# Token sums moved from VectorE to GpSimd, and the first block's groups cut as 4, 6, 6 and 6 chunks, in a two-layer diffusion backbone

## What is computed

```
for l in range(DEPTH):                                   # DEPTH = 2
    sh1, sc1, g1, ... = split(silu(c) @ w_mod[l] + b_mod[l])   # nine vectors of 1024, for latents and context
    x   = x   + 0.5 * g1  * swiglu(modulate(x, nw[0], sh1, sc1),   ffn1_up[l], ffn1_down[l])
    ctx = ctx + 0.5 * cg1 * swiglu(modulate(ctx, nw[0], ch1, cs1), ffn1_up[l], ffn1_down[l])
    ... token mixer: gated linear attention and window pooling, gates, w_out ...
    x   = x   + 0.5 * g3  * swiglu(modulate(x, nw[2], sh3, sc3),   ffn2_up[l], ffn2_down[l])
def swiglu(h, w_up, w_down):                             # w_up: 1024 x 5632, w_down: 2816 x 1024
    a, b = split(h @ w_up); return (silu(a) * b) @ w_down
```

## Time and profile before

| what | us |
|---|---|
| median of 3 runs | 2830.38 (2829.36 to 2835.23) |
| the profiled execution's own time | 2831.64 |
| its span from the first to the last instruction | 2829.4 |
| TensorE matmul busy | 2784.5 (98%) |
| VectorE busy | 1962.4 (69%) |
| ScalarE busy | 975.0 (34%) |
| GpSimd busy | 532.4 (19%) |

### The profile page before, as it was taken

One profiled execution on the slowest core, in us unless ns is written; L12 is line 12 of the kernel. 1 busy time (PEld: TensorE's weight loads), 2 busy tenths in 40 slices (PEclk: granted clock), 3 DMA queues, 4 the chain that ended last, 5 costly groups with the idle time before them and its releaser, 6 DMA issues.

```text
span 2829.4 us, 40890 instructions
## 1 busy us (share of the span) xinstructions
PE 2784.5 (98%) x15744; PEld 2472.1 (87%) x15744; DVE 1962.4 (69%) x3220; ACT 975.0 (34%) x1543; POOL 532.4 (19%) x456
## 2 busy tenths in 40 slices
PE   7999999999999999999999999999999999999998
PEld 5899899888888888999999889898988778888886
DVE  4668889565367747988886788888856577563334
ACT  5233224354322233423233433242444332432223
POOL 1013113214500020213132213131331500200000
PEclk9999999999999999999999999999999999999999
DMA  7322433231134423233332323424223145343332
GB/s 244 103 60 81 130 105 86 69 77 45 41 94 124 122 65 101 83 105 107 102 110 83 97 72 89 126 80 131 80 58 91 42 131 153 107 132 104 92 96 79
DMA packets 463787, 275.56 MB, mean 97 GB/s; under 512 B 17610, under 2 KB 461812, under 8 KB 463604
## 3 DMA queue, kind: packets, MB, share of 16 engines
q1 hardware_dynamic: 461396, 269.09, 33.8%
q10 hardware_dynamic: 2208, 4.00, 0.4%
HBM read 270.95 MB, written 2.10 MB: 97 GB/s over the span
## 4 chain that ended last, share of the span: by engine, by line
PE 92%; DVE 3%; ACT 2%; issue 1%; DMA 1%; POOL 0%; SPq 0%; ACTq 0%; DVEq 0%; POOLq 0%
PE ps L1698 37%; PE ps L1712 19%; PE ps L1956 17%; PE ps L1963 9%; PE ps L1924 2%; PE ps L1744 2%; PE ps L1929 1%; PE ps L1039 1%; DMA wraw<-in_ffn_up 1%; PE ps L1019 1%; ACT whi L2054 1%; DVE wlo L2357 0%; ACT hhi L2119 0%; PE ps L1007 0%; DVE hlo L2499 0%
## 5 line engine op out<-in xcount | busy, mean ns | idle before, releaser
L2357 DVE TENSOR_TENSOR wlo<-wraw,whi 128x1024 fp32r<-128x1024 f32 (+2 forms) x299 | 320.3, 1076 | 259.5 <-ACT whi L2054 256.6
L2054 ACT ACTIVATE whi<-wraw 128x1024 fp32r<-128x1024 f32 (+2 forms) x291 | 269.1, 926 | 588.2 <-PE ps L1712 403.4
L1698 PE MATMUL ps<-hhi,whi 128*128 128x512 f32 x1472 | 461.2, 364 | 2.2 <-ACT whi L2054 2.2
L1698 PE MATMUL ps<-hlo,whi 128*128 128x512 f32 x1472 | 453.1, 359 | 0.0
L1712 PE MATMUL ps<-hhi,wlo 128*128 128x512 f32 x1472 | 318.4, 362 | 0.0
L1698 PEld LDWEIGHTS ps<-hhi,whi 128*128 128x128 f32 x1472 | 245.9, 189 | 48.6 <-ACT whi L2054 3.8
L1712 PEld LDWEIGHTS ps<-hhi,wlo 128*128 128x128 f32 x1472 | 244.1, 188 | 44.6 <-issue 3.2
L1698 PEld LDWEIGHTS ps<-hlo,whi 128*128 128x128 f32 x1472 | 245.4, 188 | 42.8 <-issue 0.5
L2989 POOL TENSOR_TENSOR ssum<-wraw 128x512 f32<-128x512 f32 x52 | 73.1, 1406 | 1014.4 <-PE ps L1963 367.5
L1698 PE MATMUL ps<-mhi_fast,whi 128*128 128x512 f32 (+1 forms) x912 | 236.3, 340 | 1.4 <-DVE mlo_fast L2814 1.4
L1698 PE MATMUL ps<-mlo_fast,whi 128*128 128x512 f32 (+1 forms) x912 | 234.6, 338 | 0.0
(11 more groups left out here) (310 smaller groups left out, 5709.6 us busy)
## 6 DMA issues: line engine op xcount, KB each, us to landing
wraw<-in_ffn_up SPq DMA_DIRECT2D x176, 512.0 KB, 4.2
wraw<-in_w_in SPq DMA_DIRECT2D x64, 512.0 KB, 4.1
wraw<-in_ffn_down SPq DMA_DIRECT2D x80, 384.0 KB, 4.5
wraw<-in_w_mod SPq DMA_DIRECT2D x68, 256.0 KB, 3.1
modraw<-in_w_mod SPq DMA_DIRECT2D x32, 512.0 KB, 3.7
modraw_down<-in_w_mod SPq DMA_DIRECT2D x30, 512.0 KB, 3.7
flow_first<-in_w_mod SPq DMA_DIRECT2D x86, 128.0 KB, 4.2
first_mod<-in_w_mod SPq DMA_DIRECT2D x8, 1024.0 KB, 12.0
```

The costliest lines, as they stand in the source:

```text
L1698: nc.tensor.matmul(o, whi[:, slot, k, :], a[:, k * NT + t0:k * NT + t0 + n], start=(k == 0 and a is hi), stop=False)
L2054: nc.scalar.activation(whi[:, slot2, k, n], wraw[:, slot4, k, n], ACT.Copy).then_inc(hi_split, 1)
L2357: ins = nc.vector.tensor_tensor(wlo[:, slot2, k, n], wraw[:, slot4, k, n], whi[:, slot2, k, n].bitcast(F32), ALU.subtract)
```

## The change

Three things change together.

First, block (0, 0) takes the groups 4, 6, 6, 6 like the two others: two of its hidden chunks become fast pairs. Its four first jobs now stand beside pairs 0 to 3 (`lead` is gone), three jobs move into its third down phase, one flow job and two gates jobs are gone in exchange.

Second, `t_sums` leaves VectorE's queue, where it stood in the first two pairs of the first down phase, and becomes four GpSimd instructions that are issued as soon as `raw_shifted` and `h_ready` allow, which is during the first group's up phase. `t_los` moves to the first two pairs of the down phase.

Third, the key factors `kt` of the attention are computed for the latents' 512 columns alone in layer 1, on ScalarE and VectorE.

```
-QUARTERS = ((0, 6), (6, 6), (12, 4), (16, 6))
 SHORT_FIRST = ((0, 4), (4, 6), (10, 6), (16, 6))
-FFN_JOBS = {(0, 0): (4, 0, 0, 3, 0, 0, 0, 0), (0, 1): (4, 0, 0, 3, 0, 3, 0, 0), (1, 0): (4, 0, 0, 3, 0, 3, 0, 0),
+FFN_JOBS = {(0, 0): (4, 0, 0, 3, 0, 3, 0, 0), (0, 1): (4, 0, 0, 3, 0, 3, 0, 0), (1, 0): (4, 0, 0, 3, 0, 3, 0, 0),
-FLOW_JOBS = 6
+FLOW_JOBS = 5
-GATES_SPOTS = ([(0, 2), *((i, place) for i in range(1, DC) for place in (0, 1, 2))],
+GATES_SPOTS = ([(i, place) for i in range(1, DC - 1) for place in (0, 1, 2)],
...
-    if (layer, ffn) in ((0, 1), (1, 0)):
-        return SHORT_FIRST
-    return QUARTERS if (layer, ffn) in FAST else THIRDS
+    return SHORT_FIRST if (layer, ffn) in FAST else THIRDS
...
-            add("up", layer, n, ffn, t, jobs[2 * t], parts=parts, lead=2 if t == 0 and (layer, ffn) == (0, 0) else 0,
+            add("up", layer, n, ffn, t, jobs[2 * t], parts=parts, 
...
-                nc.scalar.activation(kt[:, d, :], bsum[:, 2 * pr + d, :], ACT.Exp, scale=-1.0 / TAU).then_inc(ekt_ready, 1)
+                nc.scalar.activation(kt[:, d, 0:c], bsum[:, 2 * pr + d, 0:c], ACT.Exp, scale=-1.0 / TAU).then_inc(ekt_ready, 1)
...
-            nc.vector.tensor_tensor(kt[:, d, :], kq[:, pr, :], kt[:, d, :], ALU.mult)
+            nc.vector.tensor_tensor(kt[:, d, 0:nb * P], kq[:, pr, 0:nb * P], kt[:, d, 0:nb * P], ALU.mult)
...
             def t_los(ph, which):
                 for n in which:
                     dve.wait_ge(t_hi, 4 * (fast_ffn(ph) - 1) + n + 1)
+                    dve.wait_ge(t_summed, 4 * (fast_ffn(ph) - 1) + (3, 2, 4, 4)[n])
...
                             if makes_t(ph):
-                                if 2 * i + h < 2:
-                                    t_sums(ph, (4 * i + 2 * h, 4 * i + 2 * h + 1))
-                                t_los(ph, (((), (0,), (1, 2), ()) if short(ph) else ((), (0, 1), (2, 3), ()))[2 * i + h])
+                                t_los(ph, ((0, 1), (2, 3), (), ())[2 * i + h])
...
+            def t_sums(ph):
+                f0 = fast_ffn(ph) - 1
+                pool.wait_ge(raw_shifted, DC * (f0 + 1))
+                pool.wait_ge(h_ready[1], DC * (3 * ph["layer"] + 2 * ph["ffn"] + 1))
+                s22, s12, s11, s21 = fast_blocks(hraw[:, 0:DC // 2 * NT], hraw[:, DC // 2 * NT:])
+                for out, x0, x1, op in ((s22, s12, s22, ALU.subtract), (s12, s11, s12, ALU.subtract),
+                                        (s11, s22, s11, ALU.subtract), (s21, s11, s21, ALU.add)):
+                    t_steps.link(nc.gpsimd.tensor_tensor(out, x0, x1, op))
...
             for ph in plan:
                 fast_sums(ph)
+                if makes_t(ph):
+                    t_sums(ph)
```

More of the change, by code:

```diff
@@ L141, in add_ffn @@
             add("down", layer, DC // 2, ffn, t, jobs[2 * t + 1], parts=parts,
-                flow=((), (0, 0, 0, 2), (4, 4, 4, 2) if n < 6 else (0, 0, 0, 2), ())[t] if (layer, ffn) in FAST else (),
+                flow=((), (0, 0, 0, 2), (0, 0, 0, 2), ())[t] if (layer, ffn) in FAST else (),
                 ahead=BOTH if t == len(groups) - 1 and not end else None)
@@ L754, in fast_next @@
         return nxt if nxt["fast"] else None
-    def short(ph):
-        return groups_of(ph["layer"], ph["ffn"])[ph["third"]][1] <= DC // 2
     def makes_t(ph):
@@ L2592, in tail @@
                 norm_chunk(ph, 2 * DC)
[L2594 to L2605, removed]
             def t_los(ph, which):
@@ L2777, in body @@
                                          chunks=4 if kind == "gates" and h else DC)
-                            if fast and makes_t(ph) and short(ph):
-                                t_los(ph, (3,))
                             if fast:
@@ L2989, in fast_sums @@
                         nc.gpsimd.tensor_tensor(out, x0, x1, ALU.add).then_inc(term_sum, 1)
+            def t_sums(ph):
[6 more added lines that the diff above has]
+                    t_steps.link(nc.gpsimd.tensor_tensor(out, x0, x1, op))
+            t_steps = Steps(pool, t_summed)
             odd_chunks(0, BOTH)
```

## The result

| | us, median | range | runs |
|---|---|---|---|
| before | 2832.23 | 2829.36 to 2835.23 | 6 |
| after | 2852.13 | 2851.31 to 2854.38 | 6 |

The change makes the kernel 0.71% slower: ratio 1.0071, 95% interval 1.006 to 1.0082. The forecast was slower by 12.1 us; it is 19.9 us. The time lies 1.1 us above the range. The profiled execution of after has a span of 2849.9 us.

A forecast was written before the change was run, and what follows sets the result against it. The prediction took TensorE's stream of matmuls and its waits as the bound. Its terms, -5.7 - 0.5 + 6.0 + 6.0 + 6.3 = +12.1 us, gave 2843.7 us for the profiled execution, 2842.5 us for the median, range 2832 to 2851 us.

The forecast's parts named there:

- new groups, block (0, 0): Block (0, 0): two pairs turning fast save 5.7 us, the mean difference to its neighbours; bounds 4.2 and 6.5.
- unit 2's weights late: Block (0, 0), pair 0: unit 2's loads, now behind the job slabs, come 0.4 us late, between 0 and 2.0.
- key factors: Layer 1's attention: four VectorE instructions a third shorter save 0.5 us, between 0 and 1.3.
- waits of TensorE behind the holds, three blocks: Up phases: VectorE held by GpSimd's sums makes TensorE wait 5.9, 6.0 and 6.0 us in the three blocks.
- The first stall, at unit 3: Start of unit 3: GpSimd holds the eighth `macc`, delaying the whi split; TensorE waits 3.3 us in block (0, 1).
- The second stall: Unit 5: three held instructions in pair 1 use up 4.3 us of slack; TensorE waits 2.4 us for whi.
- The hold: VectorE beside GpSimd's 1536-column sums: each caught instruction with two SBUF inputs is held 3.4 us, bounds 0 and 3.5.
- the cover for what leaves VectorE: First down phase: removing twelve VectorE instructions, 7.0 us a block, gives nothing because VectorE's own idle time there covers them.

The follow-up runs named there:

- e1: The kernel before with the new groups and job places alone, token sums staying on VectorE: 2831.86 us, ratio 0.9999.
- e6: The kernel before with ScalarE repeating the rounding of unit 5's weights in blocks (0, 1) and (1, 0), no GpSimd work added: 2842.45 us, ratio 1.0043.
- e4: The changed kernel with the weight loads of units 2 and 3 of block (0, 0) ahead of the job slabs: 2853.24 us.
- e9: The kernel before with the new groups and block (0, 0)'s weight loads of units 2 and 3 first, sums on VectorE: 2829.49 us, ratio 0.9991.
- e5: The kernel before with the shorter key factors alone: 2831.75 us, ratio 1.0001.
- e2: The kernel before with the token sums moved to GpSimd alone, old groups kept: 2848.58 us, ratio 1.0067.
- e10: The changed kernel with one GpSimd sum per finished hidden chunk and block (0, 0)'s weight loads of units 2 and 3 first: 2833.76 us, ratio 1.0009.
- e8: The changed kernel with each GpSimd sum cut into two instructions of 768 columns: 2852.29 us, ratio 1.0072.
- e3: The changed kernel with each of the four GpSimd sums waiting for one more finished hidden chunk: 2834.52 us, ratio 1.0011.

## Why the prediction was wrong

Its direction and its mechanism hold, and half of its places: the stall at unit 5 came, the one at unit 3 did not. The change is 19.9 us where 12.1 was forecast, 7.8 too little. The time lies 9.6 us from the forecast of 2842.5; the other 1.85 us are those by which the median that the sum was added to, 2830.38 of three runs, is under that of the six. The upper end of the range was 20.6 us above the median used, so a change of 19.9 us leaves the range only by this shift; the size of the sum was wrong all the same. Term by term (measured: profile of after, and of e1 where the edit stands alone):

| term | forecast | measured |
|---|---|---|
| new groups, block (0, 0) | -5.7 | -4.3 |
| unit 2's weights late | +0.4 | +1.6 |
| key factors | -0.5 | about 0 |
| waits of TensorE behind the holds, three blocks | 5.9 + 6.0 + 6.0 = 17.9 | 4.7 + 5.2 + 5.0 = 14.9 |
| low clock behind those waits | none | 1.4 + 1.7 + 2.8 = 5.9 |
| sum | +12.1 | +18.1, of 19.9 |

- **The step that failed is the sum itself: it prices a stall of TensorE at its length.** The 17.9 us of waits were 3 too many, and the clock behind them put 5.9 on top. After minus e1, both with the new groups: 6.0 + 6.8 + 8.1 = 20.9 us in the three stretches, and 14.9 + 5.9 = 20.8. e6 shows the clock term without GpSimd.
- **What the new groups save** was taken from the neighbours' stretches (5.7); it was the pairs alone, the lower bound 4.2. The forecast took it that block (0, 0) would lose its extra waits for VectorE's sums, which were 3 of 2.0 us in all against one of 0.7 in each neighbour. In e1 it still has 3, of 1.9 us, and has the wait of 0.7 for the last hidden chunk besides. The neighbours themselves were 455.1 and 455.0 us in e1, so the difference to them fits within about 1 us; their 454.0 in one profile was taken as more exact than it is.
- **The late weights** were within the bounds 0 to 2.0, but 0.4 was chosen and the wait grew by 1.6. The two loads were issued at 52.65, behind slabs that wait until 51.69. In e4 and e9 the wait goes when they stand first.
- **The first stall, at unit 3, did not come.** It needed GpSimd to hold the port against the eighth `macc`. In block (0, 1) GpSimd's first began at 1075.94, as forecast against the shifted start, and yet the eight `macc` end unheld at 1076.62 and GpSimd's instruction is the one that grows. In block (1, 0) GpSimd's first began at 1609.42 and the eighth `macc` 0.36 us later, and it too ran unheld. Why is not shown. In block (0, 0) GpSimd's first began at 64.73, 2.7 us later than the 62.0 of the forecast, since the prologue was 1.9 us longer and unit 2 another 1.2 us later; by then the eighth `macc` was already running (to 65.02). **The second stall came at twice its size**, because all three holds then fell in pair 1, against the same slack: in block (0, 1) 4.3 us of `whi` at unit 5 in place of 2.4, and 0.9 for `wlo` of unit 3. The two errors cancel to 0.8 to 1.2 us a block, and not by luck alone: three holds less one pair's slack are 9.8 - 4.3 = 5.5 us, wherever the first of them falls.
- **The hold** was right: 3.4 us forecast for each caught instruction, 3.0 to 3.3 measured (3.99 - 0.96 the least, 3.67 - 0.34 the most). The rule of the Trainium skill that was weighed against the change, page "SBUF — State Buffer", section "Who interferes with whom", was right at 1536 columns too. The same section counts `tensor_scalar` among the operations that can contend; it has one tensor input here, and the `TENSOR_SCALAR` that take 3.6 us beside GpSimd agree.
- **Key factors and the cover for what leaves VectorE**: near nothing for the first, as e5 shows; no run isolates the second.

By medians the change splits into +0.4 us for e1, where -5.3 was forecast, and 19.5 for the rest, where 17.4 was. In e1 the two located terms leave -4.3 + 1.6 = -2.7, so some 3 us are not placed. The e1 profile, of an execution of 2833.51 us, 1.7 above the median, is longer in its prologue (1.9 us beside the wait at unit 2, a longer stretch at the low clock), in blocks (0, 1) and (1, 0) (1.1 and 0.5, with one more wait of 0.7 us for VectorE's sums in each) and after the last of them (2.4, with a granted clock of 0.91 between 2220 and 2240 us). The same places vary between kernels that are alike there: the clock between 18 and 33 us is 0.77 in the profiles of before, e2 and e5, 0.54 in e6 with the same groups, and 0.54 to 0.89 with the new ones. Whether the new order of loads or chance lengthens the prologue stays open; the interval of e1 is 2.8 us to either side.

## What to carry to other kernels

Work that is moved to an engine with idle time is not free if that engine holds a port that a busy queue needs: count for each moved instruction one held instruction of the other engine at full length, and set the sum against the slack of the pair in which they fall; one hold per pair cost TensorE 0.8 us a block here, three in one pair cost 5. Cutting the instruction shorter did not help and spreading it did, but leaving the sums on VectorE was better than either (e9 against e10). And a pause of TensorE of 3 to 5 us is to be priced at its length plus a third to a half for the clock that it loses, as in the table and in e6, while a load order changed in passing is read against the first wait that needs the load.

## What the runs showed that was not expected

- All thirteen waits of 3.1 us and more at unit 5, in after, e2, e4, e6 and e8, were followed by the low clock or ended in it. Of the six waits of 1.5 to 2.1 us for the last hidden chunk in e3 and e10, three were. Of the four waits of 2.0 to 2.2 us at unit 2 in after, e1, e3 and e8, none was. The length of the wait alone does not tell.
- In five of the twelve profiles, before among them, the clock also falls for 3 us (7 in e3) in layer 0's attention although TensorE is busy throughout: between 760 and 770 us of before the granted clock is 0.83 at 10.00 us busy. What TensorE did before it fell is mostly matmuls of one column:

```profile
759.84 1.40 PE L1046 MATMUL ps<-ones,osq 128*128 128x1 f32 x12
761.88 1.39 PE L1046 MATMUL ps<-ones,osq 128*128 128x1 f32 x12
763.58 0.84 PE L1698 MATMUL ps<-hlo,whi 128*128 128x512 f32 x2
```

In after the clock does not fall there. Where it does, 3.4 us at half the clock make the span 1.7 us longer.
- The same matmuls at the same granted clock can run at two slightly different rates. One stretch of layer 0's gates phase, cut at the same instructions, in before and in e2, which are alike there:

```profile
804.93:990.52 185.59, 185.59 (x1052) 1.00 0.46 124
```
```profile
805.81:989.07 183.26, 183.26 (x1053) 1.00 0.46 126
```

TensorE is busy throughout in both, and the one takes 1.3% longer. Why is not shown. So differences of 1 to 2 us between stretches of two single profiles, such as the 5.7 us of the neighbours, carry that much chance.
